# A down projection in seven block products, with block sums made by accumulating DMAs

## The reference, cut to what is computed

```python
        m = (jax.nn.sigmoid(gate_a) * (o_a @ W_a) + jax.nn.sigmoid(gate_b) * (o_b @ W_b))
        x = x + rmsnorm(m @ w_out[l], g_post_mix[l])
        h = rmsnorm(x, g_pre_ffn[l])
        g, u = jnp.split(h @ w_gate_up[l], 2, axis=-1)
        x = x + rmsnorm((jax.nn.silu(g) * u) @ w_down[l], g_post_ffn[l])
```

## Time and profile before

| | |
|---|---|
| median of 3 runs (lowest, highest) | 764.13 us (764.1, 764.47) |
| the profiled execution, its own time | 764.42 us |
| its span, first to last instruction | 762.5 us |
| TensorE busy | 756.0 us, 99% of the span |
| VectorE, ScalarE, GpSimd busy | 523.3, 400.7, 332.8 us |
| mean granted TensorE clock | 0.999 |

### The profile page before, as it was taken

The page is one execution under the profiler, slowest core; times in us unless marked ns, Lnnn a source line. Parts: engine busy times, 40 slices in busy tenths (PEclk is TensorE's granted clock), DMA queues, the critical chain, the costliest instruction groups (busy, mean ns, idle before and its releaser), DMA issues.

```text
span 762.5 us, 12110 instructions
## 1 busy us (share of the span) xinstructions
PE 756.0 (99%) x4314; PEld 666.0 (87%) x4314; DVE 523.3 (69%) x725; ACT 400.7 (53%) x668; POOL 332.8 (44%) x219
## 2 busy tenths in 40 slices
PE   9999999999999999999999999999999999999997
PEld 7788888888888888888889989999999999888885
DVE  4979989987566665289327667888777773444474
ACT  5763287776686776632255444555555552323243
POOL 6937365957678688234563420000000003444462
PEclk9999999999999999999999999999999999999999
DMA  9653542232222422225561124333333313313312
...
DMA packets 102732, 81.54 MB, mean 107 GB/s; under 512 B 3488, under 2 KB 91560, under 8 KB 102696
## 3 DMA queue, kind: packets, MB, share of 16 engines
...
## 4 chain that ended last, share of the span: by engine, by line
PE 98%; issue 1%; POOL 0%; DVE 0%; ACT 0%; POOLq 0%; DVEq 0%
PE ps L582 26%; PE ps L561 12%; PE ps L563 12%; PE ps L562 12%; PE ps L887 8%; PE ps L886 8%; PE ps L885 8%; PE ps L648 3%; PE ps L806 3%; PE ps L795 2%; PE ps L778 1%; PE ps L780 1%; PE ps L701 1%; PE ps L700 1%; PE ps L642 0%
## 5 line engine op out<-in xcount | busy, mean ns | idle before, releaser
L1419 POOL TENSOR_TENSOR wn_lo<-raw,wn_hi 128x1024 fp32r<-128x1024 f32 x18 | 43.1, 2396 | 236.6 <-ACT wn_hi L968 236.6
L561 PE MATMUL ps<-h_hi,w_hi 128*128 128x512 f32 (+1 forms) x320 | 123.6, 386 | 0.0
L563 PE MATMUL ps<-h_hi,w_lo 128*128 128x512 f32 (+1 forms) x320 | 121.8, 381 | 0.0
L562 PE MATMUL ps<-h_lo,w_hi 128*128 128x512 f32 (+1 forms) x320 | 121.6, 380 | 0.0
L1535 POOL TENSOR_TENSOR w_lo<-raw,w_hi 128x1024 fp32r<-128x1024 f32 x30 | 78.3, 2615 | 30.5 <-ACT w_hi L1116 30.1
L1937 DVE TENSOR_TENSOR d_lo<-act,d_hi 128x512 fp32r<-128x512 f32 x18 | 41.8, 2328 | 56.0 <-ACT d_hi L1363 56.0
L1419 POOL TENSOR_TENSOR w_lo<-raw,w_hi 128x1024 fp32r<-128x1024 f32 x20 | 48.7, 2441 | 58.2 <-ACT w_hi L968 53.1
L563 PEld LDWEIGHTS ps<-h_hi,w_lo 128*128 128x128 f32 x320 | 60.2, 188 | 11.5
L562 PEld LDWEIGHTS ps<-h_lo,w_hi 128*128 128x128 f32 x320 | 60.4, 189 | 9.8
L561 PEld LDWEIGHTS ps<-h_hi,w_hi 128*128 128x128 f32 x320 | 60.3, 188 | 9.8
L885 PE MATMUL ps<-t_hi,sum_hi 128*128 128x256 f32 x216 | 61.1, 283 | 0.0
...
## 6 DMA issues: line engine op xcount, KB each, us to landing
raw<-in_w_in SPq DMA_DIRECT2D x40, 512.0 KB, 4.5
raw<-in_w_gate_up SPq DMA_DIRECT2D x26, 512.0 KB, 3.8
raw<-in_w_down SPq DMA_DIRECT2D x22, 512.0 KB, 4.1
...
raw<-in_w_out SPq DMA_DIRECT2D x8, 512.0 KB, 4.4
...
x_in<-in_x SPq DMA_DIRECT2D x4, 512.0 KB, 7.1
```

The costliest lines, as they stand in the source:

```text
L561: mm(acc, whi_c, a_hi_, start=first, stop=False)
L562: mm(acc, whi_c, a_lo_, start=False, stop=False)
L563: return mm(acc, wlo_c, a_hi_, start=False, stop=last)
L1419: nc.gpsimd.tensor_tensor(lo[:, at(u), :], raw[:, at((d % 2) * 2 + u), :], hi[:, at(u), :], sub).then_inc(w_lo_done, 1)
```

## The change

The first 18 of the 22 down tiles are no longer multiplied one by one. They are seen as nine pairs of tiles, so the product is a 2 x 2 block product: the activations have blocks by tile of the pair (`k`) and by token half, the weights by tile of the pair (`k`) and by column half (`d`). Seven products of block sums (Strassen's scheme in Winograd's form) take the place of eight. One product (`down_product(k, ...)`) has 9 tiles of depth, 256 tokens (two blocks) and 512 columns: 9 x 2 x 3 = 54 matmuls of 128 x 512. It is worked in three groups of three tiles (`GROUP = 3`), so there are 21 groups, n = 0 to 20, with 18 matmuls each. The four tail tiles are done as before.

What each engine does for a group n (k = n // 3 is its product, g = n % 3 its place in it and its slot in a ring of three):

- ScalarE, `operands_hi(n)`: copies 128 x 1536 weights to `wr_hi` and 128 x 768 activations to `xd_hi`. It waits until TensorE has done group n - 3, which frees the slot, and until the weight block is there.
- VectorE, `operands_rest(n)`: `wr_lo`, 128 x 1536. In products 2 and 5 it also makes the activation sum `x_fly`, 128 x 768 (`fly_sum`), and before group 3 three sums `t2n`, 128 x 768.
- GpSimd, `x_rest(k)`: `xd_lo`, 128 x 768, for the three groups of product k.

Of the weights SyncE loads three blocks plainly (`w_a11`, `w_a12`, `w_a22`), in three DMAs of 128 x 3 x 512 each. The block sums are made by DMAs that add onto what lies in SBUF (`accum_op=ALU.add`), issued by GpSimd in `added`: `added(0)` adds onto `w_a11` for product 5, `added(1)` adds onto `w_a22` for product 3, `added(2)` adds onto `w_a22` once more for product 4, `added(3)` adds `w_a22` onto `w_a12` for product 6. Each is three DMAs, one for each g. Output block sums are made in PSUM, by `kept` on ScalarE and a few VectorE operations. Two matmuls (`marked`) write banks 0 and 2 in product 0, for each of which `kept` then puts a copy of product 0.

Line numbers of the changed kernel differ from those of the kernel before. The core of the diff:

```diff
+        def block(dst, d, k, nth):
+            for g in range(3):
+                if nth:
+                    sp.wait_ge(block_in[g], 16 * nth)
+                sp.dma_start(group_of(dst, g), w_group(d, k, g)).then_inc(block_in[g], 16)
+        sp.wait_ge(product_done, 7 * (SEVENS - 1) + 1)
+        block(w_a11, 0, 0, 0)
+        sp.wait_ge(product_done, UP_PRODUCTS)
+        block(w_a12, 0, 1, 1)
+        block(w_a22, 1, 1, 2)
+        for i in range(LAST):
+            sp.dma_start(tail_raw[i][:, :], w_down[0][(FC - LAST + i) * P:(FC - LAST + i + 1) * P, :]).then_inc(raw_in, 16)
+        sp.wait_ge(group_done, 21)
+        sp.dma_start(g_out_row[:, :], g_post_ffn[0:1, :].partition_broadcast(P)).then_inc(g_out_in, 16)
...
+        def down_product(k, banks, first, ready=None, before=None):
+            for g in range(3):
+                s = (3 * k + g) % 3
+                pe.wait_ge(parts_lo_done, UP_PARTS + 3 * k + g + 1)
+                pe.wait_ge(x_lo_done, 3 * k + g + 1)
+                if before:
+                    before(g)
+                for b in range(2):
+                    if ready and g == 0:
+                        ready(b)
+                    for c in range(GROUP):
+                        x_h, x_l = (x[s][:, c, b * P:(b + 1) * P] for x in (xd_hi, xd_lo))
+                        w_h, w_l = (w[s][:, c, :] for w in (wr_hi, wr_lo))
+                        for n, (x_, w_) in enumerate(((x_h, w_h), (x_h, w_l), (x_l, w_h))):
+                            ins = mm(bank(banks[b]), x_, w_, start=first and g == 0 and c == 0 and n == 0,
+                                     stop=g == 2 and c == GROUP - 1 and n == 2, skip_group_check=True)
+                    if b:
+                        ins.then_inc(group_done, 1)
+                    elif g == 2:
+                        ins.then_inc(product_done, 1)
+        main, first_out, second_out, third_out = (5, 7), (0, 2), (4, 6), (1, 3)
+        def marked(g):
+            if g == 2:
+                pe.wait_ge(act_done, FC + 2)
+                for b in first_out:
+                    mm(bank(b), xd_hi[g][:, 0, 0:P], wr_hi[g][:, 0, :], start=True, stop=True)
+        pe.wait_ge(act_done, FC + 1)
+        down_product(0, main, True, before=marked)
+        down_product(1, first_out, False, lambda b: pe.wait_ge(product_kept, UP_KEPT + 1 + b))
+        down_product(2, third_out, True)
+        down_product(3, second_out, True)
+        down_product(4, main, False)
+        down_product(5, main, False, lambda b: pe.wait_ge(product_kept, UP_KEPT + 5 + b))
+        down_product(6, second_out, False, lambda b: pe.wait_ge(summed_up, UP_SUMMED + 1 + b))
+        pe.wait_ge(summed_up, UP_SUMMED + 6)
+        def activations(i):
+            pe.wait_ge(d_hi_done, i + 1)
+            pe.wait_ge(d_lo_done, i + 1)
+        block_by_block(T_END, wd_hi, wd_lo, [(tail_hi[:, i, :], tail_lo[:, i, :]) for i in range(LAST)],
...
+        def operands_hi(n):
+            k, g = n // 3, n % 3
+            if n == 0:
+                sc.wait_ge(parts_lo_done, UP_PARTS)
+            elif n == 1:
+                sc.wait_ge(product_done, UP_PRODUCTS - 1)
+            elif n == 2:
+                sc.wait_ge(product_done, UP_PRODUCTS)
+            else:
+                sc.wait_ge(group_done, n - 2)
+            if k < 3:
+                sc.wait_ge(block_in[g], 16 * (k + 1))
+            else:
+                sc.wait_ge(block_added[g], {5: 16, 3: 32, 4: 48, 6: 64}[k])
+            run(wr_hi[g][:, :, :], group_of(w_plain[k], g), ACT.Copy).then_inc(parts_hi_done, 1)
+            sc.wait_ge(sum_made, UP_SUMS + g + 1 + {2: 6, 4: 3, 5: 9}.get(k, 0))
+            run(xd_hi[g][:, :, :], x_plain[k](g), ACT.Copy).then_inc(parts_hi_done, 1)
+        def kept(k, b, dst, src):
+            if b == 0:
+                sc.wait_ge(product_done, UP_PRODUCTS + k + 1)
+            else:
+                sc.wait_ge(group_done, 3 * k + 3)
+            run(dst, bank(src), ACT.Copy).then_inc(product_kept, 1)
...
+        for n in range(1, 21):
+            operands_hi(n)
+            if n == 4:
+                for b in range(2):
+                    kept(0, b, bank(2 * b), 5 + 2 * b)
+            if n == 14:
+                for b in range(2):
+                    kept(3, b, p5_down[:, b, :], 4 + 2 * b)
+            if n == 16:
+                for b in range(2):
+                    kept(4, b, u_down[:, b, :], 5 + 2 * b)
+        for b in range(2):
+            sc.wait_ge(summed_up, UP_SUMMED + 1 + b)
+            kept(5, b, u_down[:, b, :], 5 + 2 * b)
+        sc.wait_ge(raw_in, 16 * T_END)
+        for g in range(3):
+            sc.wait_ge(block_added[g], 64)
         for i in range(LAST):
-            c = FC - LAST + i
-            sc.wait_ge(raw_in, (T_DOWN + c) // 2 * 32 + 32)
-            run(wd_hi[:, i, :], raw[:, (T_DOWN + c) % 4, :], ACT.Copy).then_inc(w_hi_done, 1)
-            run(h_hi[:, i, :], act[:, c, :], ACT.Copy).then_inc(d_hi_done, 1)
+            run(wd_hi[:, i, :], tail_raw[i][:, :], ACT.Copy).then_inc(w_hi_done, 1)
+            run(tail_hi[:, i, :], act[:, FC - LAST + i, :], ACT.Copy).then_inc(d_hi_done, 1)
...
+        def added(nth, dst, src, split_before):
+            for g in range(3):
+                gp.wait_ge(parts_lo_done, UP_PARTS + 3 * split_before + g + 1)
+                if nth:
+                    gp.wait_ge(block_added[g], 16 * nth)
+                gp.dma_start(group_of(dst, g), src(g), accum_op=ALU.add).then_inc(block_added[g], 16)
+        def x_rest(k):
+            for g in range(3):
+                n = 3 * k + g
+                gp.wait_ge(parts_hi_done, UP_PARTS + 2 * n + 2)
+                nc.gpsimd.tensor_tensor(xd_lo[g][:, :, :], x_plain[k](g), xd_hi[g][:, :, :], sub).then_inc(x_lo_done, 1)
+        x_rest(0)
+        added(0, w_a11, lambda g: w_group(1, 0, g), 0)
+        x_rest(1)
+        x_rest(2)
+        added(1, w_a22, lambda g: w_group(1, 0, g), 2)
+        x_rest(3)
+        added(2, w_a22, lambda g: w_group(0, 0, g), 3)
+        x_rest(4)
+        added(3, w_a12, lambda g: group_of(w_a22, g), 1)
+        x_rest(5)
+        x_rest(6)
         for i in range(LAST):
-            t = T_END - LAST + i
-            gp.wait_ge(w_hi_done, t + 1)
-            nc.gpsimd.tensor_tensor(wd_lo[:, i, :], raw[:, t % 4, :], wd_hi[:, i, :], sub).then_inc(w_lo_done, 1)
+            gp.wait_ge(w_hi_done, T_DOWN + i + 1)
+            nc.gpsimd.tensor_tensor(wd_lo[:, i, :], tail_raw[i][:, :], wd_hi[:, i, :], sub).then_inc(w_lo_done, 1)
...
+        def first_x_sum(g):
+            ve.wait_ge(act_done, 2 + 2 * GROUP * (g + 1))
+            tt(act_group(0, 1, g), act_group(0, 0, g), act_group(0, 1, g), sub).then_inc(sum_made, 1)
+        def second_x_sum(g):
+            ve.wait_ge(sum_made, UP_SUMS + g + 1)
+            stt(group_of(t2n, g), act_group(0, 1, g), -1.0, act_group(1, 1, g), ALU.mult, sub).then_inc(sum_made, 1)
+        def fly_sum(n, k):
+            g = n % 3
+            ve.wait_ge(group_done, n - 2)
+            ve.wait_ge(sum_made, UP_SUMS + 4 + g)
+            stt(x_fly[g][:, :, :], group_of(t2n, g), -1.0, act_group(k, 0, g), ALU.mult, sub).then_inc(sum_made, 1)
+        def operands_rest(n):
+            g = n % 3
+            ve.wait_ge(parts_hi_done, UP_PARTS + 2 * n + 1)
+            tt(wr_lo[g][:, :, :], group_of(w_plain[n // 3], g), wr_hi[g][:, :, :], sub).then_inc(parts_lo_done, 1)
+        for g in range(3):
+            first_x_sum(g)
+        operands_rest(0)
         up_2(p, 1)
         gate_two(p, 1)
         finish_pair(p, 1)
-        with ve.Fori(1, (FC - LAST) // 2) as j:
-            rest_act(j)
+        for n in range(1, 21):
+            if n == 3:
+                ve.wait_ge(product_done, UP_PRODUCTS)
+                for g in range(3):
+                    second_x_sum(g)
+            if n // 3 == 2:
+                fly_sum(n, 1)
+            if n // 3 == 5:
+                fly_sum(n, 0)
+            operands_rest(n)
+            if n == 17:
+                for b in range(2):
+                    ve.wait_ge(product_kept, UP_KEPT + 5 + b)
+                    tt(bank(4 + 2 * b), bank(4 + 2 * b), u_down[:, b, :], ALU.add).then_inc(summed_up, 1)
+        for b in range(2):
+            ve.wait_ge(product_kept, UP_KEPT + 7 + b)
+            stt(bank(1 + 2 * b), bank(1 + 2 * b), -1.0, u_down[:, b, :], ALU.mult, sub).then_inc(summed_up, 1)
+            stt(bank(5 + 2 * b), bank(5 + 2 * b), -1.0, p5_down[:, b, :], ALU.mult, sub).then_inc(summed_up, 1)```

On GpSimd, in the down stage, the kernel before runs a loop over pairs of tiles and then the tail. Rows give the line, the operation, output and inputs, shape and what it waits for:

```order
L1594 UNCONDITIONAL_BRANCH
L1594 ISA
L1419 ISA [waits w_hi_done]
L1419 TENSOR_TENSOR wn_lo<-raw,wn_hi 128x1024
L1418 REGISTER_ALU
L1419 ISA [waits w_hi_done]
L1419 TENSOR_TENSOR wn_lo<-raw,wn_hi 128x1024
L1594 REGISTER_ALU
L1594 COMPARE_AND_BRANCH
```

(28 more changed lines are left out.)

141 lines of the change are left out of this document (76 added, 65 removed).

## The result

The changed kernel takes 776.5 us (median; 776.29 to 778.99) against 764.24 us for the kernel before in the same comparison. The ratio is 1.0168, with an interval of 1.015 to 1.0185: slower by 12.3 us. The profiled execution took 776.48 us, its span is 774.7. The predicted time was 772.0 in a range of 762 to 784, so the sign and the kind of loss were right and the size was 4.5 us short. The 776.5 lies just above the likeliest case (766 to 776), towards the rival of slower sums (779).

A forecast was written before the change was run, and what follows sets the result against it. TensorE was taken to bound the kernel from end to end. Savings of 12.2 us against 0.45, start, stalls and small waits gave +6.0; clock 2 made +8: 764.4 to 772.4, so 772 us, range 762 to 784.

The forecast's parts named there:

- the likeliest case: Whole kernel: block sums land at doubled-reading speed and stall products 3 and 4; 766 to 776 us, chance 0.47.
- the rival of slower sums: Block sums: first landing 9.2 us after issue, or GpSimd issues of some us; 779 to 785 us, chance 0.2.
- What leaves TensorE (-11.8): Down stage: 432 matmuls become 378, 12.2 us less, and two `marked` matmuls add 0.45; without waits -11.8 us.
- The start of the stage (+1.8): First groups of the down stage: operands late by 0.8 us at group 1 and 1.0 at group 3.
- L = 5.9: Block sums: time from GpSimd's issue to landing of the first of three DMAs, 5.9 us with doubled reading.
- r = 4.5: Block sums: time between landings of a sum's DMAs, 4.5 us if source and destination are read in turn.
- The stalls (+6.5, +7.1): TensorE waits for block sums: 6.5 us before product 3, 7.1 before product 4.
- Groups 10, 11, 13, 14 (+1.6): Products 3 and 4: later sum parts land slower than TensorE's pace; 0.8 us for each pair of groups.
- The clock (+2, bounds 0 to 8): TensorE after stalls: half clock, absorbed behind the first stall, counting behind the second; 2 us, bounds 0 to 8.
- The tail and the kept copies (0): Tail tiles ready just as needed, 0 us (bounds 0 to 2); `kept` copies hide in a product's 12.2 us.
- plain speed: Block sums land as quickly as plain loads, 3.7 us after issue; 762 to 764 us, chance 0.2.
- the waits are not there: Order of issue or turn-taking was misread, so the waits do not occur: -11.8 to -8, 752 to 756 us, chance 0.06.

The follow-up runs named there:

- Experiment 10: The changed kernel with the three DMAs of `added(0)` issued behind the `xd_lo` of product 1, not ahead of them: 772.08 us, ratio 1.0106.
- experiment 2: The changed kernel with GpSimd's twelve DMAs copying the same bytes instead of adding: 769.41 us (one run).
- experiment 8: The changed kernel with 16 and 20 extra 128 x 128 matmuls before groups 3 and 9: 775.86 us, ratio 1.0158.
- experiment 3: The changed kernel with each part of `added(1)` and `added(2)` issued behind its own group's `xd_lo`: 765.06 us, ratio 1.0002.
- 5: The changed kernel with `t2n` sums behind `wr_lo` 3, 4, 5 and `added(1)`, `added(2)` issued part by part: 761.3 us, ratio 0.9959.
- experiment 6: The changed kernel with `t2n` sums behind `wr_lo` 3, 4, 5 and all four `added` sums issued part by part: 759.07 us, ratio 0.9934.
- 9: As experiment 6, but SyncE loads the four tail tiles only when TensorE has done 16 groups: 758.99 us, ratio 0.9927.
- 7: As experiment 6, but ScalarE's `kept(4)` copies stand one group earlier, behind group 15's operands: 759.82 us, ratio 0.994.
- the kernel without sums: The changed kernel without the four `added` calls and all waits on `block_added`, so products 3 to 6 use plain blocks: 755.57 us (one run).

## Why the prediction was right, and where its sizes were off

- **What leaves TensorE (-11.8)** was right: 52 matmuls less, 0.227 apart wherever nothing is waited for.
- **The start of the stage (+1.8)** is the step that failed most. It was 0.36 + 4.47 of gaps and 2.8 of slow matmuls behind them, 7.6 in all. Two parts of it were wrong. "`added(0)` costs nothing" looked at the block it makes, which has time, and not at GpSimd, where three issues stand ahead of group 3's `xd_lo`. Experiment 10 puts that at 4.4 us of the time, 5.4 of the stage. And the three sums were priced at 0.95 each in turns with GpSimd, but took 6.0 without the issues nearby and 10.3 with them. The prediction had named "GpSimd's issue takes so long that the first groups wait too" as a way to be wrong, and put no price on it.
- **L = 5.9** was 7.5 to 7.7. The issue takes 1.3, not 0.33 (which was SyncE's); the fixed part 2.4, not 1.1; the moving 3.8, not 4.5. **r = 4.5** was 3.8: a plain load at a full share goes at about 400 GB/s, not 350, so doubled it is 3.8. The doubled reading itself was right (experiment 2). The Trainium skill, "Collectives: The Full Stack", section "The bandwidth ceiling: the fold count and why AG ≠ RS ≠ AR", has a reduce run at about half the rate of a copy, since its add reads two sources. It says so of collectives; here the trace agrees for a DMA that adds in SBUF, 206 against 389 to 422 GB/s. The Trainium skill, "DMA: Bandwidth & Descriptors", Anatomy of one DMA, has about 2.0 us and the bytes over 436 GB/s, an estimate of 3.8 us for one part. The trace does not agree: from issue to the next copy it is 5.2 us for a copy issued by GpSimd and 7.5 for a sum, and the measurement decides.
- **The stalls (+6.5, +7.1)** were 5.58 and 6.13. L was larger by 1.6, but at the first of them the late start had moved TensorE's end of product 2 by 6.4 us (682.67 = T0 + 45.4, not 39.0) and the issue by only 4.1 (T0 + 38.4, not 34.3). So: 38.4 + 7.5 + 5.1 - 45.4 = 5.6. That this is near 6.5 is in part luck, since an L too small by 1.6 met an issue that stands 7.0 us ahead of TensorE's end of product 2, and not 4.7. The prediction let the issue come at the pace of GpSimd and VectorE. It came at TensorE's: ScalarE's copy for group 8 waited for the slot of group 5, as the row below shows, and the issue stands 5.1 behind its start, in experiments 8 and 10 too (668.00 and 673.15, 665.48 and 670.63). TensorE ends product 2 three groups behind group 5, so the stall does not depend on how late the stage started.

```profile
670.47 1.49 ACT L1467 ACTIVATE wr_hi<-w_a 128x1536 fp32r<-128x1536 f32 x1 [1.49 <-PE ps L1014]
```

- **Groups 10, 11, 13, 14 (+1.6)** did not wait: r = 3.8 is under TensorE's 4.08 a group. **Product 5's pace (+0.8)** was about 0.3.
- **The clock (+2, bounds 0 to 8)** was reckoned as the loss behind product 4's stall alone, and there it was 1.8. The 1.7 behind product 3's stall is absorbed, as argued (experiment 8); reckoned in this way the stall before product 4 is not 6.13 but 6.13 + 1.7 = 7.8, to be held against the +7.1. What was missing is the 2.8 behind the gap at the start, which no later stall swallowed (experiments 8 and 10).
- **The tail and the kept copies (0)** were right. The kept copies do cost 1.2 to 2.3 us once the larger stalls are gone (experiments 3, 5, 6, 9), and moving one only moves the wait (7).

In all, by the prediction's terms: -11.8 + 7.6 (start, clock included) + 5.6 + 7.8 + 1.8 (clock) + 1.2 (the rest) = 12.2, where it had -11.8 + 1.8 + 6.5 + 7.1 + 2 and 2.4 of small waits. Of the rivals, plain speed is out: experiment 2 shows the half rate, and even plain copies at this place in the program leave the kernel 5.0 us slower than before. The rival of slower sums erred less than it may seem: an issue takes GpSimd 1.3 us, and L is 7.5 to 7.7, between the 5.9 of the likeliest case and its 9.2. The case "the waits are not there" (752 to 756) is approached and not reached when every sum is issued part by part: experiments 6 and 9 are 0.7% faster than the kernel before, within 3.5 us of the kernel without sums.

Two things stay open. Whether the issue of a DMA on GpSimd itself holds back VectorE was not settled. In the changed kernel the second `t2n` took 2.6 us with little but issues on GpSimd beside it, and as long in experiment 2, whose issues are shorter. In experiment 6, subtractions of VectorE beside such issues ran at their own 1.75. And the width of experiment 3's runs has no cause shown.
